# Two expert layers and the step between them: weights by halves of k, gathers by quarters, one gather and one wait less

## The reference

```python
def first_block(...):                       # attention, then 64 experts of width 256, 8 per token
    ...
    h2 = modulate(rms_norm(x, norm2_g[l]), shift2, scale2)
    y = moe_ffn(h2, w_router, router_bias, w_gate_e, w_up_e, w_down_e, w_gate_sh, w_up_sh, w_down_sh)
    x = x + gate2[:, None, :] * y
    return rms_norm(x, final_g)
...
    return routed + swiglu(xt, w_gate_sh, w_up_sh, w_down_sh)     # the shared expert
...
def second_block(...):                      # conv + latent attention, memory attention, 16 experts of width 1024
    u = h @ w_in[l]
    xc, gb, gc, cq, ckv, kr, glog = jnp.split(u, splits, axis=-1)
    ...
    x = x + memory_cross_attention(rmsnorm(x, norm_mem_g[l]), rmsnorm(mem, norm_memkv_g[l]), ...)
    x = x + expert_choice_moe(rmsnorm(x, norm_moe_g[l]), ...)     # every expert takes its 32 best tokens
    return rmsnorm(x, norm_final_g)
```

## Time and profile before

| | us |
|---|---|
| median of 3 runs | 1609.52 |
| lowest and highest | 1607.74 and 1613.19 |
| profiled execution | 1612.41 |
| its span | 1610.3 |
| PE busy in the span | 1341.2 (83%) |
| DVE, ACT busy | 555.3, 404.3 |

### The profile page before, as it was taken

The page is one execution under the profiler, slowest core; times in us unless marked ns, Lnnn a source line. Parts: engine busy times, 40 slices in busy tenths (PEclk is TensorE's granted clock), DMA queues, the critical chain, the costliest instruction groups (busy, mean ns, idle before and its releaser), DMA issues.

```text
span 1610.3 us, 22428 instructions
## 1 busy us (share of the span) xinstructions
PE 1341.2 (83%) x9066; PEld 850.7 (53%) x9066; DVE 555.3 (34%) x1218; ACT 404.3 (25%) x623; POOL 68.5 (4%) x140
## 2 busy tenths in 40 slices
PE   6999999899998889988889999999666556566555
PEld 2878997545654444444578999999412112112112
DVE  2526775443323132232374665754301001001001
ACT  3437753111111110111154336453300000000001
POOL 1940000000000000000000000000000000000000
PEclk9999999999999999999989999999798887878888
DMA  9895259599999999999943443546999999999996
GB/s 351 280 301 208 105 207 401 222 413 381 379 418 385 416 420 399 416 393 405 377 176 125 157 144 126 203 159 234 371 415 415 421 415 415 422 416 416 422 416 254
DMA packets 126233, 523.33 MB, mean 325 GB/s; under 512 B 12520, under 2 KB 16768, under 8 KB 84672
## 3 DMA queue, kind: packets, MB, share of 16 engines
q1 hardware_dynamic: 121424, 518.68, 81.4%
q0 software_dynamic: 4576, 2.95, 0.8%
q10 hardware_dynamic: 144, 0.44, 0.1%
HBM read 520.96 MB, written 1.06 MB: 324 GB/s over the span
## 4 chain that ended last, share of the span: by engine, by line
PE 60%; DMA 22%; SPq 11%; DVE 3%; issue 2%; ACT 1%; DVEq 0%; ACTq 0%; PEldq 0%
PE psum L1913 18%; PE psum L2335 10%; DMA ring<-in_w_up_e_dram 9%; SPq L627 8%; DMA ring<-in_w_exp_up_dram 7%; DMA ring<-in_w_exp_down_dram 5%; PE psum L2289 4%; PE psum L2383 3%; SPq L623 2%; PE psum L2278 2%; PE psum L2755 2%; PE psum L2001 2%; PE psum L2145 1%; PE psum L1926 1%; PE psum L2619 1%
## 5 line engine op out<-in xcount | busy, mean ns | idle before, releaser
L1913 PE MATMUL psum<-arena_r,ring_r 128*128 128x256 f32 x2496 | 308.4, 284 | 12.6 <-issue 4.9
L1913 PEld LDWEIGHTS psum<-arena_r,ring_r 128*128 128x128 f32 x2496 | 299.8, 190 | 21.5 <-issue 14.5
L2335 PE MATMUL psum<-ring,arena 128*32 128x512 f32 (+1 forms) x1152 | 190.7, 638 | 33.5 <-DMA ring<-in_w_up_e_dram 25.9
L1084 DVE TENSOR_TENSOR ring_r<-ring,ring_r 128x1024 fp32r<-128x1024 f32 x140 | 162.9, 1220 | 94.5 <-ACT ring_r L726 93.8
L2755 PE MATMUL psum<-ring,arena 128*32 128x512 f32 x736 | 104.1, 702 | 62.7 <-DMA ring<-in_w_exp_up_dram 60.4
L726 ACT ACTIVATE ring_r<-ring 128x1024 fp32r<-128x1024 f32 x140 | 137.1, 1050 | 52.5 <-DMA ring<-in_w_in_dram 38.2
L2335 PEld LDWEIGHTS psum<-ring,arena 128*32 128x32 f32 (+1 forms) x1152 | 59.2, 128 | 147.7 <-issue 146.7
L2773 PE MATMUL psum<-ring,arena 128*32 128x512 f32 x384 | 67.0, 833 | 51.1 <-DMA ring<-in_w_exp_down_dram 49.0
L2755 PEld LDWEIGHTS psum<-ring,arena 128*32 128x32 f32 x736 | 22.6, 120 | 137.6 <-DMA ring<-in_w_exp_up_dram 92.8
L2383 PE MATMUL psum<-ring,arena 128*32 128x512 f32 (+1 forms) x576 | 92.9, 609 | 2.1 <-DVE arena L1487 2.1
L1852 DVE TENSOR_TENSOR arena<-arena,psum 128x256 f32<-128x256 f32 x16 | 6.7, 421 | 247.0 <-ACT arena L1043 247.0
(11 more groups left out here) (404 smaller groups left out, 1445.1 us busy)
## 6 DMA issues: line engine op xcount, KB each, us to landing
ring<-in_w_gate_e_dram SPq DMA_DIRECT2D x64, 1024.0 KB, 12.8
ring<-in_w_up_e_dram SPq DMA_DIRECT2D x64, 1024.0 KB, 14.8
ring<-in_w_down_e_dram SPq DMA_DIRECT2D x64, 1024.0 KB, 15.1
ring<-in_w_exp_down_dram SPq DMA_DIRECT2D x96, 512.0 KB, 15.7
ring<-in_w_exp_gate_dram SPq DMA_DIRECT2D x46, 1024.0 KB, 26.2
ring<-in_w_exp_up_dram SPq DMA_DIRECT2D x46, 1024.0 KB, 26.0
ring<-in_w_in_dram SPq DMA_DIRECT2D x19, 2048.0 KB, 9.3
ring<-in_w_ada_dram SPq DMA_DIRECT2D x12, 2048.0 KB, 14.0
```

The lines of the kernel that those rows point to most:

```text
L1084: V.tensor_tensor(lo, whole, hi.bitcast(F32), ALU.subtract).then_inc(w_low, 1)
L1913: ins = product(lambda a_, b_, k, first, last: mm(ps[:, t * T:(t + 1) * T], a_[:, k, c], b_[:, k, :], start=first, stop=last), w, x, None ...
L2335: ins = mm(psum[c, 5, :], xg1[:, k, P * j + width * b:P * j + width * (b + 1)], gate[e][:, :, k, :], start=(k == 0), stop=(k == KT - 1))
```

## The change

In words, by place:

- First expert layer, ring: a slot of gate and up weights no longer holds one expert with all of k but two experts with half of k: four DMAs of 512 KiB with 4 KiB rows. The first slot (or, in a quad, the first two) is released after k tile 3, and the second is waited for only before k tile 4. `used_a` no longer counts the shared expert's slot (`NU`).
- Entry of that layer: the fixed experts' columns are taken from the tables directly, so DVE makes `rows_low` and the first one-hots before it orders the experts. ACT, not DVE, copies the turned tables and the first four gathers. The ordering's matmuls (`order_items`) stand between the halves of pass 0's gates, two of the eight pieces of the shared expert stand after them, and slot 5 waits for "shu", now in the middle of pass 0.
- The last round's gather, which fetched tokens that no pass reads, is dropped, as are its one-hots. The shared expert's down product becomes a piece of pass 22. The memory's pieces move from passes 7, 8, 10, 13, 16, 17, 19, 22 to 7, 8, 10, 11, 13, 14, 16, 19.
- Mixer entry: "cq" and "ckv" are accumulated together, pair of k tiles by pair, as each pair's operands appear; the squares on ACT come after all four splits.
- `row_rstd_act`: one square root on ACT and a reciprocal on DVE.
- Second expert layer: the gather goes in four quarters, each followed by the products of its two k tiles for the first expert.

```diff
-PIECE_AT = {_p: _u for _u, _p in enumerate((7, 8, 10, 13, 16, 17, 19, 22))}
+PIECE_AT = {_p: _u for _u, _p in enumerate((7, 8, 10, 11, 13, 14, 16, 19))}
+DOWN_SH_AT = 22
+NU = NA - 1
...
+            def released(m, i):
+                if m == RING - 1:
+                    full(sp, "shu")
+                else:
+                    sp.wait_ge(used_a, i + ((NA if m < RING else NU) + m - RING + 1))
...
-                dst = ring[:, (NA + c) % RING, :].rearrange("p (g k f) -> p g (k f)", g=2, k=KT)
-                for g, w in enumerate(("w_gate_e", "w_up_e")):
-                    sp.dma_start(dst[:, g], a[w][0, e].rearrange("(p k) f -> p (k f)", p=P)).then_inc(done, 16)
+                dst = ring[:, (NA + c) % RING, :].rearrange("p (e g k) -> p e g k", e=2, g=2)
+                for j, e in enumerate((e0, e1)):
+                    for g, w in enumerate(("w_gate_e", "w_up_e")):
+                        src = a[w][0, e].rearrange("(p k) f -> p (k f)", p=P)
+                        sp.dma_start(dst[:, j, g], src[:, k * FF1:(k + KT // 2) * FF1]).then_inc(done, 16)
...
+            copy_out("tabT", rT[0:64, :], full(act, "tabT")[0:64, :])
+            for q in range(4):
+                act.wait_ge(gathered, q + 1)
+                A(xg1[:, 2 * q:2 * q + 2, 0:T], psum[:, 4 + 3 * (q % 2), :]..., ACT.Copy).then_inc(g_copied, 1)
...
+                if j < 2:
+                    high(kb, (2 + j,))
+            for j in range(4):
                 squares_of_x(j, act_squares)
...
-                A(row_rstd, row_rstd, ACT.Ln).then_inc(row_step, 1)
-                act.wait_ge(row_step, n + 1)
-                A(row_rstd, row_rstd, ACT.Exp, scale=-0.5).then_inc(row_ready, 1)
+                A(row_rstd, row_rstd, ACT.Sqrt).then_inc(row_step, 1)
...
+            step(V.tensor_scalar(items[:, 0, :, 0:FIXED], fixed(rk), -FAR, None, ALU.add))
+            step(V.tensor_copy(items[:, 1, :, 0:FIXED], fixed(wts)))
+            after_step()
+            for j in range(4):
+                rows_low(j)
+            onehots([(0, FULL, 0), (2, FULL, P)])
...
-                if j >= 1:
-                    low_gained(j - 1)
-                if j == 1:
-                    low_part(kb, (2, 3))
-            low_gained(3)
+                if j < 3:
+                    low_part(kb, (j + 1,))
+                low_gained(j)
...
                 for k in range(KT):
+                    if k == KT // 2:
+                        for s in range(gu // 2, gu):
+                            arrived_moe1(pe, m + s, turn_i)
+                    if p == 0 and k % 2 == 0:
+                        pe.wait_ge(g_copied, k // 2 + 1)
+                    if p == 0 and k == 4:
+                        order_items()
+                        onehot_turn(0, 1)
                     for b, e in enumerate(blocks):
...
-                ins.then_inc(used_a, gu)
+                    if k % 4 == 3:
+                        ins.then_inc(used_a, gu // 2)
...
+                    if p == 0:
+                        whole_piece(ps_u, w_up, hT, 2)
                     gu_turns()
+                    if p == 0:
+                        done(whole_piece(ps_u, w_up, hT, 3), "shu")
...
+                if not late and p + i3 == DOWN_SH_AT:
+                    shared_down()
...
-            project("cq", w, ("h4", 0), 0, arriving=SPLIT_AT[("b", 0)])
-            ps = start("ms34")
...
+            for q in range(4):
+                pe.wait_ge(x_low, 4 * PART_AT["h4"] + q + 1)
+                pe.wait_ge(w_low, 4 * SPLIT_AT[("b", 0)] + q + 1)
+                if q == 3:
+                    ps = start("ms34")
...
                     for c in range(4 * e, 4 * e + 4):
+                        if e == 0:
+                            if c:
+                                gather(c, gathered2)
+                            pe.wait_ge(g2_copied, i * 4 + (4 * n + c + 2))
```

264 lines of the change are left out of this document (138 added, 126 removed).

## The result

| | before | after |
|---|---|---|
| median, us | 1611.07 (5 runs) | 1601.32 (5 runs) |
| lowest and highest | 1607.74 and 1613.19 | 1600.05 and 1604.16 |
| span of the profiled execution | 1610.3 | 1599.5 |

The ratio is 0.995, 95% interval 0.9936 to 0.9964, which is 8 us (6 to 10). The medians differ by 9.75 us and the spans by 10.8, where 20 were forecast. The direction was right. The size was not, and the time lies just above the range that ended at 1601.0.

What follows compares the result with a forecast made beforehand. The weight stream was taken to bound both expert layers. Gains of 14.5 (first layer), 0.5 (mixer entry) and 5.0 us (second layer) sum to 20.0, taking the median from 1609.5 to 1589.5; range 1580 to 1601.

Steps and rivals of the forecast that it cites:

- Entry of the first layer: First expert layer's start: gates at about 287, shared piece done at 300.5; PE gains 6 us, the stream itself nothing.
- The gaps close: First expert layer: earlier slot release and PE's lead make the stream gapless, where 18.8 us of stream were lost.
- the gaps kept in part: Rival, first expert layer: slots still kept too long or SP's queue waits; half of 18.8 us remains, 1599; 14%.
- the change that does less than it says: Rival: a wait in the first layer's new entry holds PE some 10 us, half the gaps stay; 1609; 8%.
- The rate, the step that failed first: First layer's half-row slots: 409 GB/s against 421, 5.13 us a slot against 4.98; 60 x 0.15 = 9 us lost.
- The rate and the arrival of a full stream: First layer: gapless from 302.0 to 781.6, 8 KiB rows at 421 GB/s, last down slots landed 1.1 us later.
- The end of the layer: First expert layer: last down product ends at about 787, before at 801.8; 14.5 us gained.
- From the profile to the median: Whole kernel: 20.0 us off the profiled 1612.4 gives 1592.4, off its median 1609.5 gives 1589.5.
- free half rows: Rival, first expert layer: half rows cost nothing, 9 us more gained, part of it held by PE; 1581; 8%.
- Halves that stream badly: Rival, first layer: DMAs skipping every other 4 KiB run slower; gain gone at 384 GB/s, near 1622 at 370; 6%.
- Mixer entry: Mixer's start: DVE sets the pace, its chain at 827.3 against 829.0; 0.5 us gained, bounds -1.5 to 1.7.
- Second expert layer: Its entry: first slot issued 4.4 to 6.1 us after the gather starts, before 11.1; gap closes, 5.0 us, at least 3.5.

Runs made afterwards that it cites:

- whole_k: The changed kernel with whole experts in slots again, all slots of a pass awaited before its gates and released together after them: 1605.15 us (ratio 0.9969).
- rows8: The changed kernel with each gate and up slot filled by one whole expert, 8 KiB rows, two 1 MiB DMAs (wrong weights): 1589.44 us (ratio 0.9878).
- rows4_big: rows8 with every row arriving as two of 4 KiB, DMAs still 1 MiB, source read without skips: 1600.05 us (ratio 0.9929).
- small_even_odd: Against a kernel with gates and ups in separate slots (8 KiB rows), each 1 MiB DMA split into even and odd partitions: 1590.03 us (ratio 0.9881).
- mixer_old: The changed kernel with the mixer's entry as before (cq, column sums, ckv one after another, squares between the splits): 1601.42 us (ratio 0.9958).
- moe2_halves: The changed kernel with the second expert layer's gather by halves again, all ahead of the first products: 1605.68 us (ratio 0.9977).
- small_dmas: Against a kernel with gates and ups in separate slots, each 1 MiB DMA split into partitions 0 to 63 and 64 to 127: 1944.29 us (ratio 1.2081).

## Why the prediction was right and wrong, point by point

- **Entry of the first layer.** The gates of pass 0 began at 285.15 (forecast 287), slot 5 was issued at 298.8 (300.5), pass 1's gates at 302.6 (304.4). Right, and 1.7 to 1.9 us better throughout.
- **The gaps close.** Right: 407 GB/s after the quad, DMA share 1.02, and whole_k brings the gaps back when the halves are undone. The rival with the gaps kept in part is out, and so is the change that does less than it says. Among its reasons the first of them names a slow clock of PE in the 20 us after a quad; the row for 500 to 520 us has 1.00, and the slow stretch of that trace is the window 480 to 500 ahead of it, with 0.83. "No dip" was not quite right: the window 540 to 560 has 381 GB/s.
- **The rate, the step that failed first.** The sum took 0.15 us more for a slot of half rows, 60 x 0.15 = 9 us. From the issue of slot 5 to the start of the last down product the changed kernel takes 492.0 us, rows8 477.9: 14.1 us by these two profiled executions, 11.9 by the medians. Over 320 to 760 us 410 GB/s was measured where 411 to 414 was forecast. So the term was 3 to 5 us too small. Its mechanism, the length of the rows, is the larger part and was sized about right (rows4_big: 8.7 us by the profiles, 10.6 by the medians). What the sum put at nothing is what else a slot by halves brings, four DMAs and a source with skips: 5.4 us by the profiles, 1.3 by the medians.
- **The rate and the arrival of a full stream, the step that failed second.** The forecast has 482.2 us for that stretch, 473.2 of them without the cost of the rows. rows8, which has no short gate rows, takes 477.9, 4.7 more. These are not gaps, since its DMA share is 1.01. Its mean over 320 to 760 us is 419 and not 421, which makes 2.1 us. The rest, 2.6, is not shown by a run. An estimate places most of it at the end: the stream of rows8 flows from about 302.9, 94.5 slots at 419 GB/s take it to 775.9, and the last down product starts 3.4 us later, where the sum took 1.1 from the w_in load.
- **The end of the layer.** 787 was forecast and 795.8 measured: 1.7 us won at the restart, 5.0 lost in the half slots, 4.7 in the stream that was taken as perfect, and 0.7 because the last product took 5.0 us and not 4.3. Of 14.5 us 6.0 are left.
- **From the profile to the median.** The sum gives 1592.4 for the profiled execution and takes off 2.9 us for the median. The changed kernel's profiled execution is its median, 1601.3. So of the 11.8 us between 1589.5 and 1601.3 the steps above make 8.9, and 2.9 are this step, which says nothing of the kernel.
- **Why the free half rows were not worth 1581.** That rival credited 9 us for rows without cost and gave 1581; rows8 has them and stands at 1589.4. The same 4.7 us are missing there, and 2.2 of the rest are again the step from the profile to the median: rows8's profiled execution lies 0.7 above its median, not 2.9. That it equals the forecast of 1589.5 is chance.
- **Halves that stream badly.** This rival named what the sum left out, that a slot by halves costs more than its row length, but its size was far off: the effective rate of the half slots is 2.097 MB/(4.98 + 14.1/60) = 402 GB/s, and the 20 us would be gone at 384. Whether the skipped source or the four DMAs make the extra is not shown; in small_even_odd twice the DMAs with 8 KiB rows cost nothing.
- **Mixer entry.** 0.5 forecast, 0 measured (mixer_old). DVE's scaling came 4.4 us earlier (829.05 to 824.67 us) because a low part stands before it, as the prediction had it, but PE's chain behind it moved by the 6.0 us of the layer's end.
- **Second expert layer.** 5.0 forecast, 4.4 measured by moe2_halves and 4.9 in the profile (the end of the span moved by 10.8, the last load ahead of that layer by 5.8, 1135.20 to 1129.37). Right.
- **Earlier stream.** The prediction said that at the restart PE's lead counts and not the stream. The later runs confirm it more sharply than I believed when I wrote their expectations. But it also counted on PE's lead of 6 us to keep the stream running, and whole_k, which has that entry and the 13 us less of PE's work, has the gaps: it is the early release that closes them.

The sum in order, by the spans: 14.5 became 6.0, 0.5 became -0.1, 5.0 became 4.9; 20.0 became 10.8.

## What to carry to other kernels

When a stream bounds a stage, cut its slots along a dimension that leaves the rows in memory whole. The early release was worth 15.7 us here, and slots by halves of k, with their short rows, took 11.9 of them back; the same release with whole rows (gates in one slot, ups in the next) kept nearly all of it, because PE's additional loads hid. A window's DMA share tells the two apart: under 1 the stream stands still, at 1 with a lower rate it runs more slowly. And before a stream is started earlier, look at the first engine that works on it: as long as that engine never waits for weights, there is little to gain from an earlier stream (0 to 2 us here for 7 to 12).

## What the runs showed of the hardware that was not expected

- Where most DMAs write only partitions 0 to 63 or only 64 to 127, the stream runs at 251 GB/s in the mean and near 225 for long stretches (684 to 708 us of small_dmas), with the DMA engines busy, even though both kinds stand in the queue in turn. With even and odd partitions it runs at 419.
- Halving the DMAs from 1 MiB to 512 KiB with the same rows costs nothing in a full stream (1590.0 against 1591.5 us), although it adds 16 small packets for each DMA.
- 4 KiB rows cost 0.14 to 0.18 us for each 2 MiB slot against 8 KiB rows (rows4_big against rows8, 8.7 us by the profiles and 10.6 by the medians for 60 slots), about the 0.15 that the second layer's down weights had let expect. Slots by halves of k cost 0.20 to 0.23 (11.9 and 14.1 us).
- 64 fp32 products of 256 columns on 32-wide blocks take as long as 32 of 512 columns, 3.66 against 3.64 us (the records of a half quad pass), so the weight loads stay hidden at half the columns.
